# First mixer: row totals divided out on GpSimd ahead of the transposes, in a two-block transformer kernel

## The chip, the cores and the metric

One core of a Trainium2 chip runs the whole program. The metric is the device time of one execution in microseconds (us); the kernel before took 2069.79 us (median of 3 runs, 2069.43 to 2070.5).

## What is computed

The input is one sequence of 512 rows of width 1024. It goes through a first block of two layers and a second block of one layer. Every layer has a mixer (attention with 12 heads of 64 values, or a relative of it, and 4 heads of cross attention over 256 memory rows) and feed-forward parts. The change is in the mixer of the first layer, and there in the softmax of both kinds of head:

```python
def causal_block_attention(q, k, v, log_decay=None):
    ...
        logits = jnp.einsum('bhqd,bhkd->bhqk', qc, k).astype(jnp.float32)
        ...
        p = jax.nn.softmax(logits, axis=-1).astype(v.dtype)
        return jnp.einsum('bhqk,bhkd->bhqd', p, v)

def memory_cross(qm, k_mem, v_mem, q_gain, k_gain):
    ...
    p = jax.nn.softmax(logits, axis=-1).astype(v_mem.dtype)
    return jnp.einsum('bhsm,bmhd->bshd', p, v_mem).reshape(b, s, MEM_WIDTH)
```

## The kernel before

All matrix products with weights are done in three passes: each factor is split into a high part of the type fp32r and the remainder, and high by high, low by high and high by low are summed in PSUM. The weights come in units of four 128x128 tiles (RAW, by DMA), ACT makes the high part (WH, L2387) and DVE the remainder (WL, L2101). In the first mixer the projections from the normed input are steps called "wide" (L1944 to L1946, 256 columns a matmul) and the output projection `w_out` is a row of steps called "dense" (L1926 to L1928, 512 columns a matmul, three matmuls for one weight tile).

Attention is done in jobs of two heads (class `Pair`). The first mixer has eight jobs: two on the memory (two units each, of two 128-row query tiles by 256 keys) and six causal ones (three units each: query tiles 0 and 1 with 128 and 256 keys, tile 2 with 384, tile 3 with 512 keys). That is 22 units. A unit goes through these steps, for the heads x = 0 and 1:

- `pscore` (PE): scores into two PSUM banks (L2025 and L2032, the causal mask at L2015);
- `pmax` (DVE, L2211): the negated maximum of each row;
- `pexp` (ACT, L2457): the exponents into the buffer PP (four of them in turn) and, by the accumulator read that goes with each, the row totals into PSTAT;
- `pturn` (PE, L2044): transposes of 128x128 blocks of PP into the banks that held the scores. Head x waits for the exponents of head x;
- `pcopya` (DVE, L2233) and `pcopyb` (ACT, L2464): the transposed blocks into PT (two buffers);
- `pvals` (PE, L2058): values times PT, summed in PSUM bank 6, 64 array columns for each head.

Once the last unit of a job has its exponents, the division by the totals is made ready: `precip` (DVE, L2243) takes 8 reciprocals, `pwide` (GpSimd, L2622) spreads them over a 128x512 tile, `pbcast` (PE, L2068) transposes that tile in four blocks into a PSUM bank, `pspread` (ACT, L2480) copies it to TMP, `pmul` (DVE, L2248) multiplies bank 6 by it, ACT rounds the product into AOH (L2469) and `pmix` (DVE, L2251) leaves the remainder in AOL. AOH and AOL are the right-hand side of `w_out`. The other two mixers use the same classes.

The order of the program is made in two stages. `Pairs.run` is a generator: for each unit it gives out the scores of unit n+1, then the values of unit n-1, then the transposes of unit n, and `beat` interleaves this with the projection's steps at a set pace (0.65 beside the projections from the input, 1.5 beside `w_out`). Steps that follow are put off by `after`. Then the class `Arranged` goes through all steps with a cost for each (the class `Trial`) and rearranges PE, DVE and ACT: of the next 6 parts of PE (16 of DVE and ACT, 1 of GpSimd) it takes one that can begin, keeping steps of one kind in order. For PE it takes the earliest in the list that begins at most 0.15 us late by its costs. The result is a fixed order; on the chip every engine works through its own in order. The cost of a copy on GpSimd is 0.1 + n/650 us there, and a signal from GpSimd is counted as landing after 0.2 us.

Of the kernel before, what the change touches and what calls it, by code (L numbers as in the profile page):

```python
# [9 lines left out]
ALU = mybir.AluOpType  # L10
ACT = mybir.ActivationFunctionType
# [182 lines left out]
class Trial:  # L194
# [49 lines left out]
        return self.took(0.12 + size_of(out) / 960)  # L244

    def tensor_scalar(self, out, a, x, y, op0, op1=None):
        return self.took(0.12 + size_of(out) / 960)

    def tensor_reduce(self, out, a, axis, op, negate=False):
# [242 lines left out]
class Step:  # L492
# [37 lines left out]
    "pspread": ("pspread.act",),  # L530
    "pmul": ("pmix.mul", "pmix.act"),
    "pmix": ("pmix.dve",),
    "memload": (),
    "project": ("project.dve",),
    "conv": ("conv.act", "conv.dve"),
# [29 lines left out]
def program(nc, io):  # L565
    with ExitStack() as ctx:
# [471 lines left out]
        class Pairs:  # L1038


            def __init__(self, jobs, free):
                self.jobs, self.free, self.at = jobs, free, {}
                self.id = n_att[0]
                n_att[0] += 1

# [9 lines left out]
            def score(self, n, u):  # L1055
                job, key, jkey = self.jobs[n], (self.id, n, u), (self.id, n)
                if u == 0:
                    pstats.take(jkey, [("pwide.pool", jkey)])
                self.at[key] = t = Unit(job.units[u], pick_pair(att_ring), job.spare)
                held.update(t.banks)  # L1060
                for x, b in enumerate(t.banks):
                    psum.take(("pscore", key, x), [("pexp.act", key + (x,))], b)
                step("pscore", key, job=job, u=u, t=t)
                S, tokens = PSTAT[pstats.of[jkey]], pstats.before[jkey]

                def rest():
                    need(job.roots[1] if job.roots else [])
                    for xs in ((slice(0, 2),) if t.joint else (slice(0, 1), slice(1, 2))):
                        step("pmax", key + (xs.start,), job=job, t=t, xs=xs, S=S, tile=key, before=tokens)
                    if job.sealed(u) and job.sink is not None:  # L1070
                        step("psink", jkey, job=job, S=S, last=key + (0 if t.joint else 1,))
                    after(0.8 if job.spare else 0, exponents)

                def exponents():
                    free = []
                    for n_ in range(t.parts):
                        t.P.append(pp.take(("pp", key, n_), [("pturn.pe", key + (x,)) for x in range(2) if t.shared or x == n_]))
                        free += pp.before["pp", key, n_]
                    for x in range(2):
                        step("pexp", key + (x,), job=job, t=t, x=x, S=S, P=t.of(PP, t.P, x), before=tokens, src=PS[t.banks[x]],  # L1080
                             turned=free, top=("pmax.dve", key + (0 if t.joint else x,)))
                after(0.4, rest)
                return 0.4 + 1.4 * t.width / 512

            def turn(self, n, u):
                job, key = self.jobs[n], (self.id, n, u)
                need([("pexp.act", key + (1,))])
                t = self.at[key]
                t.copied = [("pcopy.act", key + (1,))] + ([] if t.shared else [("pcopy.dve", key + (0,))])
                for n_, b in enumerate(t.banks[0:t.parts]):  # L1090
                    psum.take(("pturn", key, n_), t.copied if t.shared else [x for x in t.copied if x[1][-1] == n_], b)
                for x in range(2):
                    step("pturn", key + (x,), t=t, P=t.of(PP, t.P, x), out=t.of(PS, t.banks, x),
                         before=psum.before["pturn", key, x] if x < t.parts else [])
                held.difference_update(t.banks)

                def copies():
                    if job.sealed(u):
                        self.recip(n)
                    free = []  # L1100
                    for n_ in range(t.parts):
                        t.PT.append(pt.take(("pt", key, n_), [("pvals.pe", key)]))
                        free += pt.before["pt", key, n_]
                    if t.shared:
                        both = lambda bufs, at: bufs[at[0]][:, :].rearrange("p (x k) -> p x k", x=2)[:, :, 0:t.width]
                        step("pcopyb", key + (1,), src=both(PS, t.banks), dst=both(PT, t.PT), free=free, turned=key + (1,))
                    else:
                        for x in range(2):
                            step(("pcopya", "pcopyb")[x], key + (x,), src=t.of(PS, t.banks, x), dst=t.of(PT, t.PT, x), free=free,
                                 turned=key + (x,))  # L1110
                after(0.5 if job.spare else 0.6, copies)
                return 0.25 * t.width / 128

            def values(self, n, u):
                job, key, jkey, ckey = self.jobs[n], (self.id, n, u), (self.id, n), (self.id, self.jobs[n].chunk)
                t = self.at[key]
                need(t.copied)
                if u == 0:
                    psum.take(("pvals", jkey), [("pmix.mul", ckey)], 6)
                step("pvals", key, job=job, u=u, jkey=jkey, t=t)  # L1120
                return 0.3 * t.width / 128

            def sums(self, n, i):
# [20 lines left out]
            def mix(self, n):  # L1144
# [4 lines left out]
                step("pmul", key, last=self.end(n), F=F, h=h, free=free)  # L1149
                after(1.2, lambda: step("pmix", key, F=F, h=h, l=l))  # L1150

            def older(self, scored, turned):

                ends = turned and self.jobs[turned[0]].sealed(turned[1])
                late = ends and self.jobs[turned[0]].spare
                cost = self.sums(*turned) if ends and not late else 0
                cost += self.values(*turned) if turned else 0
                cost += self.turn(*scored) if scored else 0
                return cost + (self.sums(*turned) if late else 0)
# [381 lines left out]
        for p in range(6):  # L1541
# [1 line left out]
            jobs.append(Pair([(qh[r, :], ql[r, :]) for r in (lo, hi)], [(kh[r, :], kl[r, :]) for r in (lo, hi)],  # L1543
                             VP[p // 2 % 2][:, :, 128 * (p % 2):128 * (p % 2) + 128], CAUSAL, p, pair_got[p],
                             cum=(2 * p, 2 * p + 1), wants=3))
        att = Pairs(jobs, fox_free)
        atts.append(att)
        side.append(att.run())
        pace[0], aux_ring[:] = 0.65, [2, 3, 4, 5, 7]
# [360 lines left out]
        def tensor(pe):  # L1910
            w = pe if trial(pe) else Once(pe)
            for s in turns(pe, "pe"):
# [125 lines left out]
                elif k == "pturn":  # L2038
                    for t in a["before"]:
                        w.wait_ge(*done(*t))  # L2040
                    w.wait_ge(*done("pexp.act", key))
                    for x in range(a["t"].width // 128):
                        c = slice(128 * x, 128 * x + 128)
                        p = pe.transpose(a["out"][:, c], a["P"][:, c], IDENT)  # L2044
# [40 lines left out]
        def vector(dve):  # L2085
# [6 lines left out]
            for s in turns(dve, "dve"):  # L2092
# [136 lines left out]
                elif k == "pcopya":  # L2229
                    for t in a["free"]:  # L2230
                        w.wait_ge(*done(*t))
                    w.wait_ge(*done("pturn.pe", a["turned"]))
                    dve.tensor_copy(a["dst"], a["src"]).then_inc(done.sem("pcopy.dve"), 1)  # L2233
                elif k == "precip":
                    St = a["S"]
                    for x in range(2):
# [138 lines left out]
        def scalar(act):  # L2375
# [3 lines left out]
            for s in turns(act, "act"):  # L2379
# [80 lines left out]
                elif k == "pcopyb":  # L2460
                    for t in a["free"]:
                        w.wait_ge(*done(*t))
                    w.wait_ge(*done("pturn.pe", a["turned"]))
                    act.activation(a["dst"], a["src"], ACT.Copy).then_inc(done.sem("pcopy.act"), 1)  # L2464
                elif k == "pmul":
                    for t in a["free"]:
                        w.wait_ge(*done(*t))
# [78 lines left out]
        def gpsimd(pool):  # L2546
# [31 lines left out]
            for s in turns(pool, "pool"):  # L2578
# [25 lines left out]
                elif k == "krope":  # L2604
                    w.wait_ge(*done("rtab.pool", 0))
                    w.wait_ge(*done(*a["got"]))
                    A, B = (x[:, :, :].rearrange("p (t h) f -> p t h f", t=4)[:, :, 0, :] for x in MLA_ROT)
                    M = [RS[x][:, 0:128].rearrange("p (t f) -> p t f", t=4) for x in range(2)]
                    turned(KRT[:, :, :], A, B, M, KRO[:, :, :]).then_inc(done.sem("krope.pool"), 1)
                    w.wait_ge(*done("krope.pool", 0))  # L2610
                elif k == "trope":
                    w.wait_ge(*done("rtab.pool", 0))
                    for t in a["got"]:
                        w.wait_ge(*done(*t))
                    w.wait_ge(g_in.sem, g_in.n)
                    turned(a["y"], a["A"], a["B"], a["M"], a["y"]).then_inc(done.sem("trope.pool"), 1)
                    w.wait_ge(*done("trope.pool", key))
                elif k == "pwide":
                    for t in a["before"]:
                        w.wait_ge(*done(*t))  # L2620
                    w.wait_ge(*done("precip.dve", key))
                    pool.tensor_copy(a["inv"][:, :].rearrange("p (i x d) -> p i x d", i=4, x=2),  # L2622
                                     a["S"][:, :, 3, :].rearrange("p x i -> p i x").unsqueeze(3).broadcast_to(
                                         [128, 4, 2, 64])).then_inc(done.sem("pwide.pool"), 1)
                elif k == "zero":
                    pool.memset(HX[key][:, 0:30], 0.0).then_inc(done.sem("zero.pool"), 1)

# [154 lines left out]
```

## Time and profile before

| What | Before |
|---|---|
| median of 3 runs | 2069.79 us |
| the profiled execution | 2069.65 us |
| its span, first to last instruction | 2067.9 us |
| PE busy | 2052.2 us |
| DVE busy | 1284.6 us |
| ACT busy | 966.0 us |
| GpSimd busy | 39.2 us |

The profiled execution took 0.14 us less than the median, and 1.75 us of its time lie outside its span. Matmuls are pipelined and their ends are modelled, so a matmul's row shows some 0.27 us where the next one starts 0.1 us later; the cost of a group of matmuls is read from start to start.

### The profile page before, as it was taken

Reading aid. Unit: us, or ns where it says so; the run is one execution under the profiler, and the core shown is the slowest. Engines: PE = TensorE matmul, PEld = TensorE weight load, DVE = VectorE, ACT = ScalarE, POOL = GpSimd, SP = SyncE. Lnnn points to the kernel's source line nnn. Section 1 sums busy time; section 2 is a strip of 40 time slices with the busy share of each in tenths; the row PEclk is TensorE's granted clock in tenths of the full one; section 3 lists DMA queues with packets and bytes.
Section 4 is the critical chain, followed back from the end, with each engine's and each line's share of the span. In section 5 each row is a group of like instructions: output and inputs, shape, how many; then the busy total and the mean of one; then the engine's idle time right before and its main releaser. Section 6 shows DMA issues by size and latency. Waiting matters only on the chain.

```text
span 2067.9 us, 29799 instructions
## 1 busy us (share of the span) xinstructions
PE 2052.2 (99%) x11018; PEld 1725.1 (83%) x11018; DVE 1284.6 (62%) x2111; ACT 966.0 (47%) x1883; POOL 39.2 (2%) x86
## 2 busy tenths in 40 slices
PE   8999999999999999999999999999999999999999
PEld 8998788888889788888888888888889878888887
DVE  7656688547756977774577555344548995544542
ACT  7655465334446865543344433223344764322331
POOL 0000001000000000000000000000001000000000
PEclk9999999999999999999999999999999999999999
DMA  6212233333323112333333333333332123333332
GB/s 220 68 47 62 62 97 97 97 97 97 97 90 98 45 36 63 92 99 97 96 97 98 97 96 97 97 97 97 97 94 75 37 82 95 97 98 96 98 101 87
DMA packets 101809, 185.51 MB, mean 90 GB/s; under 512 B 11552, under 2 KB 15008, under 8 KB 101408
## 3 DMA queue, kind: packets, MB, share of 16 engines
q1 hardware_dynamic: 101664, 183.61, 29.4%
q8 instruction: 87, 1.43, 0.3%
q14 instruction: 58, 0.48, 0.1%
HBM read 181.47 MB, written 2.10 MB: 89 GB/s over the span
## 4 chain that ended last, share of the span: by engine, by line
PE 97%; ACT 2%; DVE 1%; issue 0%; DMA 0%; POOLq 0%; DVEq 0%; ACTq 0%
PE PSA L1926 26%; PE PSA L1928 25%; PE PSA L1927 25%; PE PSA L1944 3%; PE PSA L1945 3%; PE PSA L1946 3%; PE PSA L2058 2%; PE PSA L2032 2%; PE PSA L2044 2%; PE PSA L1986 1%; ACT PP L2457 1%; PE PSA L2015 0%; PE PSA L2068 0%; PE PSA L2025 0%; PE PSA L1959 0%
## 5 line engine op out<-in xcount | busy, mean ns | idle before, releaser
L2387 ACT ACTIVATE WH<-RAW 128x512 fp32r<-128x512 f32 (+2 forms) x681 | 426.9, 628 | 810.6 <-PE PSA L1928 680.9
L2101 DVE TENSOR_TENSOR WL<-RAW,WH 128x512 fp32r<-128x512 f32 (+2 forms) x681 | 468.0, 688 | 390.9 <-ACT WH L2387 369.3
L1926 PE MATMUL PSA<-HNh,WH 128*128 128x512 f32 x1440 | 562.5, 391 | 0.0
L1928 PE MATMUL PSA<-HNh,WL 128*128 128x512 f32 x1440 | 560.3, 389 | 0.0
L1927 PE MATMUL PSA<-HNl,WH 128*128 128x512 f32 x1440 | 560.2, 389 | 0.0
L1927 PEld LDWEIGHTS PSA<-HNl,WH 128*128 128x128 f32 x1440 | 270.3, 188 | 57.0 <-issue 1.2
L1926 PEld LDWEIGHTS PSA<-HNh,WH 128*128 128x128 f32 x1440 | 270.3, 188 | 57.0 <-issue 1.2
L1928 PEld LDWEIGHTS PSA<-HNh,WL 128*128 128x128 f32 x1440 | 270.3, 188 | 56.4
L1926 PE MATMUL PSA<-Gh,WH 128*128 128x512 f32 x704 | 273.9, 389 | 0.0
L1927 PE MATMUL PSA<-Gl,WH 128*128 128x512 f32 x704 | 273.9, 389 | 0.0
L1928 PE MATMUL PSA<-Gh,WL 128*128 128x512 f32 x704 | 273.9, 389 | 0.0
L2124 DVE TENSOR_TENSOR PSA<-PSA,ACC 128x512 f32<-128x512 f32 x180 | 125.5, 699 | 166.6 <-PE PSA L1928 158.6
L1944 PE MATMUL PSA<-WH,HNh 128*128 128x256 f32 (+2 forms) x512 | 152.2, 297 | 6.1 <-DVE WL L2101 6.1
L1928 PEld LDWEIGHTS PSA<-Gh,WL 128*128 128x128 f32 x704 | 132.1, 188 | 27.5
L1927 PEld LDWEIGHTS PSA<-Gl,WH 128*128 128x128 f32 x704 | 132.1, 188 | 27.4
L1926 PEld LDWEIGHTS PSA<-Gh,WH 128*128 128x128 f32 x704 | 132.1, 188 | 27.4
L1945 PE MATMUL PSA<-WH,HNl 128*128 128x256 f32 (+2 forms) x512 | 148.1, 289 | 0.0
L1946 PE MATMUL PSA<-WL,HNh 128*128 128x256 f32 (+2 forms) x512 | 148.0, 289 | 0.0
L2089 DVE SCALAR_TENSOR_TENSOR CV<-PSA,PAR,CV 128x511 f32<-128x511 f32 (+1 forms) x176 | 131.9, 749 | 12.0 <-ACT CV L2486 3.4
L1944 PEld LDWEIGHTS PSA<-WH,HNh 128*128 128x128 f32 x512 | 99.0, 193 | 7.4 <-DVE HNl L2089 6.1
L1945 PEld LDWEIGHTS PSA<-WH,HNl 128*128 128x128 f32 x512 | 99.0, 193 | 0.2
L1946 PEld LDWEIGHTS PSA<-WL,HNh 128*128 128x128 f32 x512 | 98.8, 193 | 0.0
(267 smaller groups left out, 2206.5 us busy)
## 6 DMA issues: line engine op xcount, KB each, us to landing
RAW<-in_w SPq DMA_DIRECT2D x659, 256.0 KB, 2.6
XT<-in_x SPq DMA_DIRECT2D x8, 256.0 KB, 5.4
MT<-in_mem SPq DMA_DIRECT2D x2, 1024.0 KB, 5.3
out_x<-XT SPq DMA_DIRECT2D x8, 256.0 KB, 2.1
RAW<-in_w SPq DMA_DIRECT2D x8, 208.0 KB, 2.3
RAW<-in_w SPq DMA_DIRECT2D x6, 192.0 KB, 2.8
RAW<-in_w SPq DMA_DIRECT2D x8, 134.0 KB, 4.8
PAR<-in_par SPq DMA_DIRECT2D x1, 207.0 KB, 3.6
```

The lines of the kernel that those rows point to most:

```text
L1926: pe.matmul(out, wh, xh, start=(a["start"] and c == 0), stop=False)
L1927: pe.matmul(out, wh, xl, start=False, stop=False)
L1928: p = pe.matmul(out, wl, xh, start=False, stop=ends)
L1944: pe.matmul(out, h[:, c], wh, start=(a["start"] and t % a["share"] == 0), stop=False)
L1945: pe.matmul(out, l[:, c], wh, start=False, stop=False)
L1946: p = pe.matmul(out, h[:, c], wl, start=False, stop=(a["stop"] and t % a["share"] == a["share"] - 1))
L2032: p = pe.matmul(PS[tile.banks[x]][:, col:col + nk], job.q[x][qx][:, qs], job.k[x][kx][:, ks], start=(opens and n == 0 and m == 0), stop=(( ...
L2044: p = pe.transpose(a["out"][:, c], a["P"][:, c], IDENT)
L2089: ins = dve.scalar_tensor_tensor(*x)
L2101: dve.tensor_tensor(l, r, h, ALU.subtract).then_inc(done.sem("split.dve"), 1)
L2124: dve.tensor_tensor(ps, ps, nm.acc, ALU.mult).then_inc(done.sem("scale.dve"), 1)
L2387: act.activation(h, r, ACT.Copy).then_inc(done.sem("split.act"), 1)
```

## The change

In the first mixer (`Pairs(jobs, fox_free, True)`) each unit's exponents are multiplied by the reciprocals of their rows' totals in place. After both heads' exponents DVE takes the reciprocals of this unit's rows (`pshare`), then GpSimd multiplies PP by them (`pnorm`, one `tensor_scalar` for each query tile and head), and the transposes wait for `pnorm` instead of `pexp`. `precip`, `pwide`, `pbcast`, `pspread` and `pmul` are not given out there. ACT rounds bank 6 itself into AOH (`pout`) and `pmix` takes the remainder from bank 6, which is free again after `pmix` (before: after `pmul`). The two other mixers keep the steps of before. `Trial` gets a cost for `tensor_scalar` on GpSimd.

```diff
     def tensor_scalar(self, out, a, x, y, op0, op1=None):
+        if self.name == "pool":
+            return self.took(0.1 + size_of(out) / 650)
         return self.took(0.12 + size_of(out) / 960)
...
             def score(self, n, u):
...
-                    pstats.take(jkey, [("pwide.pool", jkey)])
+                    pstats.take(jkey, [("pnorm.pool", self.end(n) + (1,)) if self.early else ("pwide.pool", jkey)])
...
+                    if self.early:
+                        after(0.8, shares)
+
+                def shares():
+                    step("pshare", key, S=S, rows=t.rows)
+                    for x in range(2):
+                        step("pnorm", key + (x,), t=t, x=x, S=S, P=t.of(PP, t.P, x))
...
             def turn(self, n, u):
-                need([("pexp.act", key + (1,))])
+                need([("pnorm.pool" if self.early else "pexp.act", key + (1,))])
...
-                         before=psum.before["pturn", key, x] if x < t.parts else [])
+                         before=psum.before["pturn", key, x] if x < t.parts else [],
+                         got="pnorm.pool" if self.early else "pexp.act")
...
-                    if job.sealed(u):
+                    if job.sealed(u) and not self.early:
                         self.recip(n)
...
-                    psum.take(("pvals", jkey), [("pmix.mul", ckey)], 6)
+                    psum.take(("pvals", jkey), [("pmix.dve" if self.early else "pmix.mul", ckey)], 6)
                 step("pvals", key, job=job, u=u, jkey=jkey, t=t)
+                if self.early and job.sealed(u):
+                    after(0.2, lambda: self.out_of(n))
...
+            def out_of(self, n):
+                job, key = self.jobs[n], (self.id, self.jobs[n].chunk)
+                free = self.free(job.chunk)
+                need(free)
+                F, h, l = PSA[:, 6, :], AOH[:, job.chunk, :], AOL[:, job.chunk, :]
+                step("pout", key, last=self.end(n), F=F, h=h, free=free)
+                after(0.8, lambda: step("pmix", key, F=F, h=h, l=l))
...
-                ends = turned and self.jobs[turned[0]].sealed(turned[1])
+                ends = turned and self.jobs[turned[0]].sealed(turned[1]) and not self.early
...
-        att = Pairs(jobs, fox_free)
+        att = Pairs(jobs, fox_free, True)
...
+                elif k == "pshare":
+                    St, rows = a["S"], a["rows"]
+                    for x in range(2):
+                        w.wait_ge(*done("pexp.act", key + (x,)))
+                    dve.reciprocal(St[:, :, 3, rows], St[:, :, 1, rows]).then_inc(done.sem("pshare.dve"), 1)
...
+                elif k == "pout":
+                    for t in a["free"]:
+                        w.wait_ge(*done(*t))
+                    w.wait_ge(*done("pvals.pe", a["last"]))
+                    act.activation(a["h"], a["F"][:, :], ACT.Copy).then_inc(done.sem("pmix.act"), 1)
...
+                elif k == "pnorm":
+                    w.wait_ge(*done("pshare.dve", key[:-1]))
+                    for i, col, k0, nk, masks in a["t"].subs:
+                        z = pool.tensor_scalar(a["P"][:, col:col + nk], a["P"][:, col:col + nk],
+                                               a["S"][:, a["x"], 3, i:i + 1], None, ALU.mult)
+                    z.then_inc(done.sem("pnorm.pool"), 1)
```

## Rows read from the trace of the kernel before

**Rows 1.** The page: busy time by engine, and the chain that ended last.

```profile
PE 2052.2 (99%) x11018; PEld 1725.1 (83%) x11018; DVE 1284.6 (62%) x2111; ACT 966.0 (47%) x1883; POOL 39.2 (2%) x86
...
PE 97%; ACT 2%; DVE 1%; issue 0%; DMA 0%; POOLq 0%; DVEq 0%; ACTq 0%
```

**Rows 2.** Busy time by stretch: start:end, length, PE, PEld, DVE, ACT, POOL, PEclk, DMA, GB/s.

```profile
60.00:240.00 180.00, 180.00 (x1597) 159.30 (x1596) 108.88 (x205) 105.40 (x279) 4.91 (x8) 1.00 0.19 55
```

**Rows 3.** What PE waited for in the whole span: us, times, longest us.

```profile
PE PSA L1944 <- DVE WL L2101: 6.1, 1, 6.1
PE PSA L2044 <- ACT PP L2457: 4.4, 6, 1.9
```

**Rows 4.** Timeline of PE (start us, us, operation, count): L2068, and the values behind.

```profile
82.55 0.66 PE L2068 MATMUL PSA<-CONST,TMP 128*128 128x128 f32 x4
83.14 1.09 PE L2058 MATMUL PSA<-PT,VMEM 128*64 128x128 f32 x16
...
121.91 0.61 PE L2068 MATMUL PSA<-CONST,TMP 128*128 128x128 f32 x4
122.45 1.09 PE L2058 MATMUL PSA<-PT,VP 128*64 128x128 f32 x16
```

**Rows 5.** PE's groups of instructions from 60 to 240 us, by shape: L2068.

```profile
L2068 PE MATMUL PSA<-CONST,TMP 128*128 128x128 f32 x32 | 4.9, 275 | 0.0
```

**Rows 6.** Timeline of PE: the first wide matmul behind values, and the next two.

```profile
143.57 0.38 PE L1944 MATMUL PSA<-WH,HNh 128*128 128x256 f32 x1
...
144.03 0.28 PE L1944 MATMUL PSA<-WH,HNh 128*128 128x256 f32 x1
144.38 0.28 PE L1944 MATMUL PSA<-WH,HNh 128*128 128x256 f32 x1
```

**Rows 7.** GpSimd's groups by shape: operation, shapes, count, busy us, mean ns, idle before.

```profile
L2573 POOL TENSOR_TENSOR RT<-YC,Q_ROT 128x128 f32<-128x128 f32 x8 | 4.5, 584 | 24.2 <-ACT SQ L2429 24.2
L2598 POOL TENSOR_TENSOR Q_ROT<-TMP,PAR 128x32 f32<-128x32 f32 x16 | 4.4, 304 | 0.0
...
L2587 POOL TENSOR_SCALAR TMP<-TMP 128x96 f32<-128x96 f32 x1 | 0.5, 467 | 97.0 <-ACT TMP L2508 97.0
L2566 POOL CAST CONST<-PT 128x140 fp32r<-128x140 f32 x1 | 0.3, 303 | 0.0
```

**Rows 8.** Timelines of GpSimd and DVE: one spread copy with a subtraction beside it.

```profile
88.02 0.61 POOL L2622 COPY TMP<-PSTAT 128x512 f32<-128x512 f32 x1 [12.22 <-DVE PSTAT L2243]
88.20 0.97 DVE L2251 TENSOR_TENSOR AOL<-TMP,AOH 128x512 fp32r<-128x512 f32 x1 [0.25 <-ACT AOH L2469]
...
103.18 0.69 DVE L2251 TENSOR_TENSOR AOL<-TMP,AOH 128x512 fp32r<-128x512 f32 x1 [0.23 <-ACT AOH L2469]
```

**Rows 9.** Timeline of ACT: the last exponents of two units.

```profile
102.34 0.19 ACT L2457 ACTIVATION_READ_ACCUMULATOR PP<-PSA,PSTAT 128x1 f32 x1
...
210.50 0.20 ACT L2457 ACTIVATION_READ_ACCUMULATOR PP<-PSA,PSTAT 128x1 f32 x1
```

**Rows 10.** Timeline of PE: the transposes of these units; then the last values.

```profile
108.91 0.88 PE L2044 MATMUL PSA<-CONST,PP 128*128 128x128 f32 x6
...
210.83 1.09 PE L2044 MATMUL PSA<-CONST,PP 128*128 128x128 f32 x8
...
231.48 1.09 PE L2058 MATMUL PSA<-PT,VP 128*64 128x128 f32 x16
```

**Rows 11.** DVE's groups from 60 to 240 us: the product with the spread totals, the reciprocals.

```profile
L2248 DVE TENSOR_TENSOR TMP<-PSA,TMP 128x512 f32<-128x512 f32 x8 | 5.5, 691 | 5.0 <-PE PSA L2058 5.0
L2243 DVE RECIPROCAL PSTAT<-PSTAT 128x8 f32<-128x8 f32 x8 | 1.6, 203 | 6.7 <-ACT PP L2457 6.7
```

**Rows 12.** Timeline of DVE at the mixer's end: last remainder, two additions of projection sums.

```profile
234.11 0.68 DVE L2251 TENSOR_TENSOR AOL<-TMP,AOH 128x512 fp32r<-128x512 f32 x1
...
238.96 0.69 DVE L2257 TENSOR_TENSOR XT<-PSA,XT 128x512 f32<-128x512 f32 x1 [1.25 <-PE PSA L1928]
247.87 0.69 DVE L2257 TENSOR_TENSOR XT<-PSA,XT 128x512 f32<-128x512 f32 x1 [2.01 <-PE PSA L1928]
```

More of the change, by code:

```diff
@@ L532 @@
     "pmix": ("pmix.dve",),
+    "pshare": ("pshare.dve",),
+    "pnorm": ("pnorm.pool",),
+    "pout": ("pmix.act",),
     "memload": (),
@@ L1038, in program, with __init__ @@
         class Pairs:
-            def __init__(self, jobs, free):
-                self.jobs, self.free, self.at = jobs, free, {}
+            def __init__(self, jobs, free, early=False):
+                self.jobs, self.free, self.at, self.early = jobs, free, {}, early
                 self.id = n_att[0]
@@ L2040, in tensor @@
                         w.wait_ge(*done(*t))
-                    w.wait_ge(*done("pexp.act", key))
+                    w.wait_ge(*done(a["got"], key))
                     for x in range(a["t"].width // 128):
```

## The prediction

> **What bounds the kernel.** The page comes first: PE is busy for 99% of the span and carries 97% of the chain that ended last; DVE and ACT have a third to a half of the time free and GpSimd nearly all [rows 1]. So only what PE does, or waits for, can change the time. The second view is the table of busy time by stretch. The first mixer's attention lies between 60 and 240 us; there PE shows 180.00 of 180 us busy at full clock, DVE 108.88, ACT 105.40, GpSimd 4.91 [rows 2]. The third is the list of what PE waited for. It holds six waits of transposes for exponents, 4.4 us together, and one wait for weights of 6.1 us at the start [rows 3]. Since the second view shows no idle PE from 60 to 240 us, none of these to speak of is in the stretch that is changed. Modelled ends could cover short stalls there, so I also followed the starts on PE's timeline: between 60 and 256 us each group starts when the group before has had its usual time, and what is over are switches between full and half array (some 0.1 us each, below). PE is saturated there: work taken off it is a gain of its own size, delay elsewhere costs nothing as long as PE finds other work.
>
> **What is removed from PE.** Each of the eight jobs loses its four transposes of spread reciprocals, 32 in all [rows 5]. The cost is read from start to start: 83.14 - 82.55 = 0.59 us at one place, 122.45 - 121.91 = 0.54 us at another [rows 4]. The eight places read 0.59, 0.54, 0.54, 0.53, 0.54, 0.52, 0.53 and 0.53 us, 4.3 us together. They stand mostly between a unit's scores and an older unit's values, both of which use half the array, so the switch goes with them. **Term 1: -4.3 us.** No other step of PE is added or dropped; transposes of exponents, scores and values keep their number.
>
> **What is removed and added elsewhere.** DVE loses eight products of 0.691 us and eight reciprocals of 0.203 us, 7.1 us [rows 11]; it gets 22 reciprocals of two or four columns, at most 0.203 us each, 4.5 us. ACT loses eight copies of the spread tile. Rounding and remainder stay, with PSUM as source. All this is beside PE and costs nothing; the cover is PE's own work. GpSimd loses eight spread copies and gets 80 multiplications: for a causal job two each of 128, 256, 384 and 512 columns, for a memory job eight of 256. No DMA is moved, and none waits on these steps.
>
> **The price of one multiplication.** The trace has no such instruction of this width. From below: the spread copy of 512 columns takes 0.61 us [rows 8] and the cast of 140 takes 0.303 [rows 7], a slope of 0.31/372 = 0.83 ns a column. From above: products of two tensors take 0.304 us for 32 columns and 0.584 for 128 [rows 7], 2.9 ns a column, 1.70 us for 512. The nearest row by kind is the one multiplication by a scalar, 96 columns in 0.467 us [rows 7]; with the copies' slope that gives 0.49, 0.60, 0.71 and 0.81 us for 128, 256, 384 and 512 columns. I take these, since there is one tensor input as in a copy. A unit then costs GpSimd 2.2, 1.4 and 1.6 us (causal, in order) or 2.4 us (memory), 41 us in all over 180: it does not become the bound.
>
> The Trainium skill bears on this choice. Its page "GPSIMD Engine Reference" (Elementwise — side-by-side cycle accounting) puts ordinary elementwise work at about 2.6 cycles an element on GpSimd, a floor that it gives for two inputs, and the best loops at 1.8, with 512 elements in 769 ns. By the first figure, at the 1.2 GHz of that page, a 512-column multiplication would be an estimated 1.1 us and more, by the second close to what I took. The spread copy here, at 0.61 us for 512 columns, is quicker than both.
>
> **The new wait and who is behind it.** The transposes now wait for reciprocals and two multiplications. After the last exponents come some 0.3 us for the reciprocal with its signals and 1.4 to 2.4 us of GpSimd: about 2.4 us later than before for head 1, and more for head 0, which used to go ahead of head 1's exponents. How long did transposes lie ready? A unit in the middle has its last exponents at 102.34 + 0.19 and is turned at 108.91, 6.4 us later; one of the fifth causal job has 210.70 and 210.83, hardly anything [rows 9, 10]. Over the 22 units I count 12 with under 3 us (three of the four memory units, three of the third and fourth causal jobs, all six of the last two). There a static order as before would stall PE by about 2 us each. But the order is made anew by `Arranged`, which leaves a late transpose at the head of its six parts and takes wide or dense tiles past it. There is enough to take: the last values start at 231.48 [rows 10] and their remainder is done at 234.79, yet the first sum that needs them is added at 247.87, with twelve tiles between it and the addition at 238.96 [rows 12]. So the tail has over 10 us of cover. The stall that remains is what the planner misjudges. It counts 0.1 + n/650 us: 1.58, 1.38, 1.78 and 1.98 us a unit against my 2.2, 1.4, 1.6 and 2.4. The excess, 0.6 us for two tight first units and 0.4 for three memory units, is 2.4 us, and a late transpose falls on average into the middle of a tile, which hides most of it. **Term 2: +0.7 us** (bounds 0 and the second rival's 13).
>
> **Array switches.** Values that come ready later may no longer stand directly behind scores. Leaving a values group costs the next wide step 0.46 us (143.57 to 144.03) in place of 0.35 (144.03 to 144.38) [rows 6], and entering about the same, so a separated group costs 0.2 us. Two or three such, **term 3: +0.5 us** (bounds -0.5, if the new order joins groups, and +2, ten groups).
>
> **Other things held longer.** Bank 6 is freed by `pmix`, so after a rounding and a subtraction instead of one product: about 1.5 us later. Next values come 5 us and more after, no price. PP and score banks are kept 2.4 us longer; four PP buffers are two units, and scores of unit n+2 come after the transposes of unit n anyway. GpSimd and DVE get in each other's way: the subtraction that ran beside a spread copy took 0.97 us, not 0.69, 0.28 more for 0.43 us of overlap, and the copy kept its 0.61 [rows 8]. With 41 us of GpSimd and about a fifth of DVE's time in such two-input instructions, DVE pays some 6 us of its 71 free ones. No price, as PE's weights are split well ahead.
>
> **Sum:** -4.3 + 0.7 + 0.5 = -3.1 us. The profiled execution would go from 2069.65 to 2066.6; it stands 0.14 us under the median, so the forecast for the median is 2069.79 - 3.1 = 2066.7 us. A measurement of this kernel tells about 0.2% (4.1 us) from no change, so this counts as the same.
>
> **Rivals.**
> - *All of it is kept*: the planner's price of GpSimd is at or above the true one, no stall, no lost switch. For it: the copy is quicker than the planner counts (0.61 against 0.89). Against it: the small instructions look dearer. 2069.8 - 4.3 = 2065.5 us, just past the 0.2% line; with joined groups 2065.0. Chance 0.25.
> - *GpSimd is slow* (slower than before): a multiplication costs what a product of two tensors does. A unit is then 3.1, 2.7, 3.4 or 3.8 us, 1.3 to 1.9 us over plan, and PE, in order, waits at each of the 12 tight places: 18.6 us, less some 6 hidden in tiles, so about +13 - 4.3 = 2078 us. It decides from about 0.7 us of stall at each of 12 places, which is 1.2 to 1.3 us for 512 columns. For it: the two-tensor rows. Against it: one tensor input only. Chance 0.10.
> - *The delay eats the gain*: reciprocals stand behind other work on DVE and are slowed by GpSimd, score banks are held and PE finds the next step of its kind blocked. Half the places cost 0.7 us: +4, 2069.7 us, between 2068 and 2072. For it: the last two jobs have no slack and tight spacing. Against it: the cover counted above. Chance 0.15.
> - *The forecast*, 2065.9 to 2068: chance 0.50.
>
> That the change is without effect on PE is excluded: the 32 transposes go.
>
> **Chances and range.** Faster by over 0.2% is most of the first rival and an edge of the forecast: 0.25. Slower by over 0.2% is the second and a little of the third: 0.12. The rest, 0.63, is within. The range leaves out the second rival and a margin below the first: 2065.0 to 2072.0 us.
>
> **What would show it.** Right: L2068 has 32 matmuls less, none from 60 to 240 us; GpSimd gains about 36 us; multiplications of 512 columns take near 0.8 us; PE from 60 to 240 us has waits of under 1.5 us for GpSimd; the stretch up to the first feed-forward part ends 3 us earlier and all behind it is unchanged. Wrong: waits of transposes on GpSimd of several us, 512 columns at 1.2 us or more, or time that moves in stages after the first mixer.

## The result, and the profile after

| Kernel | Median | Ratio to before, 95% interval |
|---|---|---|
| before | 2069.79 us (5 runs, 2069.33 to 2070.50) | |
| changed | 2088.22 us (5 runs, 2086.36 to 2090.42) | 1.0085 [1.0075, 1.0096] |

The change made the kernel 18.4 us slower by the medians. The forecast was 2066.7 us, range 2065.0 to 2072.0, and slower had a chance of 0.12. The profiled execution took 2086.36 us with a span of 2084.6 us, 16.7 more than before; it was the fastest of the five, so the account below explains 16.7 us, and the other 1.7 us of the median have no trace.

The page first: busy time by engine of the changed kernel. It answers to [rows 1].

```profile
PE 2053.8 (99%) x10986; PEld 1722.1 (83%) x10986; DVE 1283.3 (62%) x2118; ACT 962.0 (46%) x1875; POOL 102.8 (5%) x142
```

PE has 32 matmuls less, as forecast. GpSimd gained 64 us where I had priced some 36. Next the table of busy time by stretch of the changed kernel (start:end, length, then PE, PEld, DVE, ACT, POOL, granted clock, DMA share, GB/s); it answers to [rows 2].

```profile
60.00:90.00 30.00, 27.70 (x260) 25.66 (x258) 20.10 (x45) 20.39 (x61) 12.93 (x13) 1.00 0.17 54
90.00:140.00 50.00, 50.00 (x482) 45.31 (x481) 28.33 (x55) 28.02 (x75) 20.71 (x20) 1.00 0.18 53
140.00:190.00 50.00, 45.84 (x421) 40.41 (x421) 24.75 (x47) 26.03 (x70) 17.46 (x16) 1.00 0.16 50
190.00:240.00 50.00, 43.94 (x311) 34.73 (x312) 26.35 (x54) 22.00 (x59) 14.14 (x14) 0.93 0.16 48
```

PE was never idle from 60 to 240 us before. Now it is idle for 2.3 us beside the memory jobs, for 4.2 beside the third and fourth causal jobs and for 6.1 beside the last two, where the granted clock is 0.93 too. From 90 to 140 us, where exponents used to lie ready for five us and more, nothing is lost. The list of what PE waited for in the changed kernel names the cause; it answers to [rows 3].

```profile
PE PSA L2067 <- POOL PP L2661: 13.3, 16, 2.2
PE PSA L1967 <- DVE WL L2124: 6.8, 2, 6.1
PE PSA L2067 <- ACT PP L2485: 4.4, 6, 1.9
PE PSA L2055 <- ACT PT L2492: 1.4, 2, 0.7
PE PSA L1967 <- DVE XT L2112: 0.8, 1, 0.8
```

L2067 are the transposes, L2661 the multiplications: 16 waits, 13.3 us. Their durations, from GpSimd's groups by shape, stand beside [rows 7].

```profile
L2661 POOL TENSOR_SCALAR PP<-PP,PSTAT 128x256 f32<-128x256 f32 x28 | 27.5, 991 | 59.7 <-DVE PSTAT L2261 59.7
L2661 POOL TENSOR_SCALAR PP<-PP,PSTAT 128x512 f32<-128x512 f32 x12 | 19.0, 1598 | 28.4 <-DVE PSTAT L2261 28.4
L2661 POOL TENSOR_SCALAR PP<-PP,PSTAT 128x384 f32<-128x384 f32 x12 | 14.8, 1242 | 7.1 <-DVE PSTAT L2261 7.1
...
L2661 POOL TENSOR_SCALAR PP<-PP,PSTAT 128x128 f32<-128x128 f32 x12 | 7.5, 628 | 66.1 <-DVE PSTAT L2261 66.1
```

512 columns take 1.60 us, not the 0.81 that I took; the slope is (1598 - 628)/384 = 2.5 ns a column. GpSimd's rows are rough, but the timeline of GpSimd, where neighbours are merged into one row from the first start to the last end, gives nearly the same: two of 512 columns in 3.10 us, four of 256 in 3.64 us, two each of 128 and 256 in 2.98 us.

```profile
83.00 3.64 POOL L2661 TENSOR_SCALAR PP<-PP,PSTAT 128x256 f32<-128x256 f32 x4 [3.25 <-DVE PSTAT L2261]
...
96.47 2.98 POOL L2661 TENSOR_SCALAR PP<-PP,PSTAT 128x128 f32<-128x128 f32 x4 [3.19 <-DVE PSTAT L2261]
...
111.72 3.10 POOL L2661 TENSOR_SCALAR PP<-PP,PSTAT 128x512 f32<-128x512 f32 x2 [4.61 <-DVE PSTAT L2261]
```

(The row at 96.47 merges both widths under the first.) Where did the time go, in place? The sum of squares for the feed-forward part stands right behind the changed stretch, and the start of its first matmuls is a mark that can be read in every kernel. PE's timeline before, then changed:

```profile
271.40 1.02 PE L1969 MATMUL PSA<-ACC,ONE 128*128 128x512 f32 x2
...
286.91 1.02 PE L1992 MATMUL PSA<-ACC,ONE 128*128 128x512 f32 x2
```

That is +15.5 us. The first matmul of the second memory projection starts at 639.8 and 656.5, +16.7; the end of the span is +16.7. So 15.5 us are lost in the changed stretch, 1.2 between the two marks, near the second mixer, and nothing later.

### The profile page after: what moved, and what is told of

It reads as the page before. It is cut to its first block, busy times and chain, and to the rows that moved or that the text cites. A ratio compares the mean times of both kernels' runs of the same rounds, so it can differ in the third digit from the quotient of the medians.

```text
span 2084.6 us, 29827 instructions
## 1 busy us (share of the span) xinstructions
PE 2053.8 (99%) x10986; PEld 1722.1 (83%) x10986; DVE 1283.3 (62%) x2118; ACT 962.0 (46%) x1875; POOL 102.8 (5%) x142
## 4 chain that ended last, share of the span: by engine, by line
PE 94%; ACT 2%; POOL 1%; DVE 1%; DMA 1%; issue 1%; SPq 0%; POOLq 0%; DVEq 0%; ACTq 0%
PE PSA L1949 25%; PE PSA L1951 25%; PE PSA L1950 25%; PE PSA L1967 3%; PE PSA L1968 3%; PE PSA L1969 3%; PE PSA L2055 2%; PE PSA L2081 2%; PE PSA L2067 2%; POOL PP L2661 1%; PE PSA L2009 1%; ACT PP L2485 1%; PE PSA L2038 0%; DVE PSTAT L2234 0%; DMA MT<-in_mem 0%
## 5 line engine op out<-in xcount | busy, mean ns | idle before, releaser
L1949 PE MATMUL PSA<-HNh,WH 128*128 128x512 f32 x1440 | 562.5, 391 | 0.0
L1949 PEld LDWEIGHTS PSA<-HNh,WH 128*128 128x128 f32 x1440 | 270.3, 188 | 57.0 <-issue 1.2
L1949 PE MATMUL PSA<-Gh,WH 128*128 128x512 f32 x704 | 273.9, 389 | 0.0
L1949 PEld LDWEIGHTS PSA<-Gh,WH 128*128 128x128 f32 x704 | 132.1, 188 | 27.4
```

The lines of the kernel that those rows point to most:

```text
L1949: pe.matmul(out, wh, xh, start=(a["start"] and c == 0), stop=False)
```

## Experiments

Each ran on the same chip as its own runs of the kernel before; ratios are given with their 95% intervals. The median of before was 2070.28 us beside one_block, short_mults, planned_true and mults_on_dve, 2070.18 beside true_reach16, dve_by_head, gpsimd_middle_jobs and dve_first_six, and 2070.14 beside changed_reach16, dve_reach16 and dve_six_reach16. Two theories stood at first: (1) GpSimd's multiplications are longer than planned for, and PE stands in its fixed order; (2) some other part of the change costs, whatever GpSimd takes.

### One block: what the removed work is worth

```diff
                 elif k == "pbcast":
...
-                    for i in range(4):
+                    for i in range(4 if trial(pe) or key[0] else 1):
```

> The kernel before in its own order, but in the first mixer only one of the four blocks of spread reciprocals is transposed (three quarters of the multiplier tile are then old PSUM contents). It prices the work taken off PE: 24 transposes of 0.107 us are 2.6 us. Theory (PE saturated, work removed is gained at its own size): 2067.2 us, ratio 0.9988. Rival (PE's pace is set by something else there): no change, 2069.8 us.

2067.69 us, ratio 0.9987 [0.9978, 0.9996]: 2.6 us less than before, by 24 transposes of 0.108 us. The mark behind the stretch agrees:

```profile
268.60 1.02 PE L1969 MATMUL PSA<-ACC,ONE 128*128 128x512 f32 x2
```

It stands 2.8 us earlier than before, so the rival (no change) is out: PE is saturated there, and work that is taken off it is gained at its own size. By 0.108 us each, 32 are worth 3.45 us. That the switch of each of the eight groups makes up the rest of the 4.3 is not shown by this run, which keeps one transpose in each group; dve_reach16, below, bears on it.

### Short multiplications in the same order

```diff
-                        z = pool.tensor_scalar(a["P"][:, col:col + nk], a["P"][:, col:col + nk],
+                        n = nk if trial(pool) else 16
+                        z = pool.tensor_scalar(a["P"][:, col:col + n], a["P"][:, col:col + n],
                                                a["S"][:, a["x"], 3, i:i + 1], None, ALU.mult)
```

> The changed kernel with the same planned order on every engine, but each GpSimd multiplication does only the first 16 columns of its query tile (the rest of the exponents stays undivided, so this leaves out most of the division). Theory 1 (GpSimd's real multiplications, 0.63 to 1.60 us, are longer than the planner's price, and PE stands still in its fixed order): each falls to 0.3 to 0.5 us, PE's waits for GpSimd fall from 13.3 us to under 1 us and the time to 2065 to 2067 us, 3 to 5 us below the kernel before. Theory 2 (another part of the change costs, whatever GpSimd takes: bank 6 held until the remainder, transposes of head 0 waiting for head 1, DVE's reciprocals): the time stays above 2078 us.

2070.72 us, ratio 1.0001 [0.9992, 1.0011]. The order of every engine is that of the changed kernel, so the length of the multiplications alone is worth 2088.2 - 2070.7 = 17.5 us: theory 1. Theory 2 wanted over 2078 us and is out. But 2065 to 2067 was missed too, since not all of the rest comes back. The lists of waits and of GpSimd's groups of this kernel:

```profile
PE PSA L1967 <- DVE WL L2124: 6.6, 2, 6.2
PE PSA L2067 <- ACT PP L2485: 4.5, 6, 1.9
PE PSA L2067 <- POOL PP L2662: 2.0, 2, 1.1
PE PSA L2055 <- ACT PT L2492: 1.4, 2, 0.7
PE PSA L1967 <- DVE XT L2112: 0.8, 1, 0.8
...
L2662 POOL TENSOR_SCALAR PP<-PP,PSTAT 128x16 f32<-128x16 f32 x64 | 23.0, 380 | 188.3 <-DVE PSTAT L2261 188.2
```

Even at 0.38 us each, the first transposes of the last two jobs wait 1.0 us each for multiplications: these begin only when both heads have their exponents, and the order put nothing in between. The mark behind the stretch in this kernel:

```profile
270.30 1.02 PE L1992 MATMUL PSA<-ACC,ONE 128*128 128x512 f32 x2
```

It is 1.1 us earlier than before. Of that, -4.3 were forecast for the removed work, +2.0 are these waits and +0.2 one for DVE at 74.7 us; by difference some +1.0 is left for array switches and waits too short to show. The 1.2 us near the second mixer come on top, and the span ends 0.1 us under that of before.

### The planner told the truth

```diff
         if self.name == "pool":
-            return self.took(0.1 + size_of(out) / 650)
+            return self.took(0.33 + size_of(out) / 410)
```

> The changed kernel with only the planner's price of a GpSimd multiplication set to what the trace shows, 0.33 + n/410 us in place of 0.1 + n/650; the instructions are the same, PE, DVE and ACT get another order. Theory 1a (the misjudged price alone cost the time; there is other work to put in): PE's waits for GpSimd under 2 us, time 2065 to 2068 us. Theory 1b (the chain through GpSimd is too long for the last two jobs; no order fills it, since projection tiles and scores stand in line behind buffers and banks that the late transposes hold): still 2073 us or more, with PE idle in the last two jobs, from about 205 to 250 us.

2081.15 us, ratio 1.0051 [1.0036, 1.0066]. Theory 1a falls: the true price takes back only 7 of the 18 us. Theory 1b fits so far. PE's timeline of this kernel ahead of the last causal job's first transposes:

```profile
226.33 0.34 PE L2055 MATMUL PSA<-FKH,FQL 64*128 64x384 f32 x2
226.60 0.28 PE L2038 MATMUL PSA<-CB 128*128 128x128 bf16 x2
230.72 0.87 PE L2067 MATMUL PSA<-CONST,PP 128*128 128x128 f32 x3 [3.84 <-POOL PP L2661]
231.24 0.77 PE L1949 MATMUL PSA<-AOH,WH 128*128 128x512 f32 x1
```

PE stands for 3.84 us before a transpose, and directly behind that transpose comes a tile of the output projection (L1949), which multiplies the outputs of older jobs. Why was it not taken first? That gave a third theory (1c): the planner's list of six parts was full of attention steps that all waited on the same chain. A list of 16 in the kernel before gives the identical program, so the length of the list by itself costs or gains nothing there.

### A longer list

```diff
-        arranged.append(Arranged(trials, ("dve", "act", "pe"), {"pe": 6, "dve": 16, "act": 16, "pool": 1}, chains))
+        arranged.append(Arranged(trials, ("dve", "act", "pe"), {"pe": 16, "dve": 16, "act": 16, "pool": 1}, chains))
```

> As planned_true (true price of the multiplications), and the planner may look 16 parts ahead on PE instead of 6. The same change of 6 to 16 in the kernel before gives that kernel's own order on every engine again, so the reach by itself changes nothing there. Theory 1c (the six parts were full of attention steps that waited, with projection tiles ready behind them): PE keeps working through the last two jobs, waits for GpSimd under 2 us, 2067 to 2072 us. Rival (the tiles behind are themselves blocked by banks, weights or the emission order): as planned_true, 2079 to 2083 us.

2069.41 us, ratio 0.9997 [0.9987, 1.0006]. What PE waited for in this kernel:

```profile
PE PSA L1967 <- DVE WL L2124: 6.1, 1, 6.1
PE PSA L2067 <- ACT PP L2485: 4.4, 6, 1.9
PE PSA L2055 <- ACT PT L2492: 1.4, 2, 0.7
PE PSA L1967 <- DVE XT L2112: 0.8, 1, 0.8
PE PSA L2067 <- POOL PP L2661: 0.8, 2, 0.5
```

Waits for GpSimd fell from 7.6 us (in planned_true) to 0.8, with multiplications as long as ever. So the longer chain can be covered, and theory 1b falls too; it was the short list that hid the cover. What stood in the six parts at each wait is not shown. The fourth combination is the low price with the long list:

> The changed kernel with only the planner's reach on PE raised from 6 to 16 parts; the price stays too low (0.1 + n/650). It completes the table of price and reach. Theory (both faults count, and reach is the larger: it let the blocked steps fill the list; the low price leaves waits of about 1 us where a transpose is placed as early as it was thought ready): between true_reach16 and the changed kernel, 2073 to 2078 us, PE's waits for GpSimd 4 to 10 us. Rival A (reach alone explains it): 2069 to 2071 us. Rival B (the low price alone decides): 2084 us or more.

2082.39 us, ratio 1.0056 [1.0042, 1.0070]; I had expected 2073 to 2078. Its waits for GpSimd are 10.9 us, in 14 places:

```profile
PE PSA L2067 <- POOL PP L2661: 10.9, 14, 2.2
```

| | list of 6 | list of 16 |
|---|---|---|
| price 0.1 + n/650 | 2088.2 | 2082.4 |
| price 0.33 + n/410 | 2081.2 | 2069.4 |

Either mend alone brings 6 to 7 us, both together 19. The reading that fits: with the low price a transpose is put in too early, however long the list; with the short list a rightly priced transpose still finds no tile to be put behind. The expectation that the reach was the larger fault was wrong: the two are of a size, and each hides the other.

### The same multiplications on DVE

```diff
-    "pnorm": ("pnorm.pool",),
+    "pnorm": ("pnorm.dve",),
...
+                        z = dve.tensor_scalar(a["P"][:, col:col + nk], a["P"][:, col:col + nk],
+                                               a["S"][:, a["x"], 3, i:i + 1], None, ALU.mult)
```

> The changed kernel with the multiplications on DVE in place of GpSimd (same steps, DVE priced at 0.12 + n/960 us by the planner). Theory 1 (the length of GpSimd's multiplications): DVE does 512 columns in 0.4 to 0.7 us, a unit costs under 1.4 us, PE waits little, 2065 to 2068 us. Theory 2 (other parts of the change): above 2075 us. If DVE gets too full, waits for WL or for maxima appear and the time lies between, 2068 to 2074 us.

2069.26 us, ratio 0.9995 [0.9986, 1.0005]. DVE's groups from 60 to 262 us of this kernel:

```profile
L2265 DVE TENSOR_SCALAR PP<-PP,PSTAT 128x256 f32<-128x256 f32 x28 | 8.8, 348 | 0.0
...
L2265 DVE TENSOR_SCALAR PP<-PP,PSTAT 128x512 f32<-128x512 f32 x12 | 5.5, 483 | 0.2
```

DVE does 512 columns in 0.48 us where GpSimd takes 1.60. With the short list and the changed kernel's steps, 19 us are back, though the 2065 to 2068 us expected were missed; 1.7 us of waits in the last two jobs remain (two, 1.0 at most), like those of the short multiplications. I tried to remove them by giving each head its own reciprocals:

> As mults_on_dve, and each head has its own reciprocal, so that head 0 is multiplied and transposed without waiting for head 1's exponents. Theory (of what is left in mults_on_dve above the sum of removed work, 1.7 us is two waits of first transposes in the last two jobs for multiplications that wait for both heads): those waits go, 2067.5 to 2068.5 us. Rival (22 more small DVE instructions take back what it gives): 2069 to 2070.5 us.

2069.07 us, ratio 0.9995 [0.9986, 1.0005], no difference that can be told: the wait before the last job's first transposes went from 0.78 us to 0.82, and that of the job before is now 0.95 us for the exponents themselves. So waiting for both heads was not what cost the time. The next kernel is mults_on_dve with the long list:

> As mults_on_dve with a reach of 16 parts. Theory (its two waits of 1.7 us before the first transposes of the last two jobs have the same cause, a full list): they go, 2067 to 2068.5 us. Rival (they come from DVE being later than planned): 2069 to 2070 us.

2068.10 us, ratio 0.9988 [0.9979, 0.9998]. By the medians alone this can't be told from mults_on_dve, but the two waits are gone, as the list of this kernel shows (DVE's multiplications are not in it):

```profile
PE PSA L1967 <- DVE WL L2124: 6.2, 1, 6.2
PE PSA L2067 <- ACT PP L2491: 4.5, 6, 1.9
PE PSA L2055 <- ACT PT L2498: 1.4, 2, 0.7
PE PSA L1967 <- DVE XT L2112: 0.8, 1, 0.8
PE PSA L2055 <- DVE PT L2256: 0.2, 1, 0.2
PE PSA L2091 <- POOL TMP L2661: 0.2, 1, 0.2
```

and the mark behind the stretch is at 267.57 us, where mults_on_dve has 269.93:

```profile
267.57 1.02 PE L1992 MATMUL PSA<-ACC,ONE 128*128 128x512 f32 x2
```

It is 3.8 us earlier than before. So the removed work is worth nearly the 4.3 us that were forecast once nothing waits, with 0.5 us left for switches; 1.2 us go again near the second mixer.

### Only some of the jobs

The flag `early` became a tuple of job numbers (0 and 1 are the memory jobs, 2 to 7 the causal ones), and `self.early` the test `n in self.early`. This kernel also has the right price, so it is compared with planned_true:

```diff
-            return self.took(0.1 + size_of(out) / 650)
+            return self.took(0.33 + size_of(out) / 410)
...
-        att = Pairs(jobs, fox_free, True)
+        att = Pairs(jobs, fox_free, (2, 3, 4, 5))
```

> GpSimd multiplications only in the first four causal jobs, with the true price in the planner; the two memory jobs and the last two causal jobs divide as before. Theory (the loss sits in the memory jobs and the last two causal jobs, which have no slack between exponents and transposes): four of the eight gains of 0.54 us are kept, less 1.2 us lost in another order near the second mixer and some 1 us of waits in the third and fourth causal job: 2069 to 2071 us. Rival (every job loses): 2075 us or more.

2070.42 us, ratio 1.0003 [0.9994, 1.0013], with 0.3 us of waits for GpSimd. With the other four jobs dividing as before, the loss of planned_true (2081.2 us) is gone: with the right price and the short list it sits in the memory jobs and the last two causal ones. With the low price the third and fourth causal jobs lose too, 4.2 us of idle PE in the changed kernel; that split was not run. The next kernel has the multiplications of jobs 0 to 5 on DVE, with the short list:

> As mults_on_dve for the first six jobs; the last two causal jobs divide as before. Six of eight gains of 0.54 us, 3.2 us, without the two waits of 1.7 us together, less up to 1.2 us near the second mixer: 2067 to 2068.5 us. Rival (the gain is lost in array switches and order all the same): 2069.5 us or more.

2067.81 us, ratio 0.9988 [0.9979, 0.9997]: six of the eight groups of transposes are gone, without the waits. With the long list as well:

> As dve_first_six with a reach of 16 parts; the version that should be best. dve_first_six shows no waits that the kernel before has not, but for 0.8 us near the second mixer, so there is little for the reach to give: 2067 to 2068.3 us, ratio 0.9985 to 0.999. Rival: the memory jobs gain too, 2066.5 us.

2067.88 us, ratio 0.9991 [0.9982, 1.0000]. The three best versions (dve_reach16, dve_first_six and this one) lie 2.0 to 2.4 us below the kernel before by their medians, two of them clear of 1 by their intervals, and can't be told from each other. The gain over the kernel before is small, 0.1%.

## Why the prediction was wrong, point by point

- **PE bounds, and removed work is gained at its own size: right.** one_block shows it for 24 of the 32 transposes. The mark of dve_reach16, 3.8 us earlier than before, bears -4.3 us out to within the 0.5 us of term 3.
- **The price of one multiplication: wrong, and the first step that failed.** I put 512 columns between 0.61 and 1.70 us and took 0.81, by the rule that one tensor input makes it like a copy. It measured 1.60, with the slope of 2.5 ns that products of two tensors suggested (2.9) and not the copy's 0.83. (The text counts 80 multiplications; its own list gives 64, and 64 ran. Its 41 us go by the 64.) The row that I trusted, 96 columns in 0.467 us, was near the truth (the new slope gives 0.55 for 96) but could not give a slope. A unit cost 3.0, 2.5, 3.1 or 3.6 us where the second rival had said 3.1, 2.7, 3.4 and 3.8; and 1.60 is past the 1.2 to 1.3 from which I had said it decides. The page "GPSIMD Engine Reference" of the Trainium skill (Elementwise — side-by-side cycle accounting) gives about 2.6 cycles an element, for two inputs, and I set that figure aside because the copy was quicker. The multiplication, with one tensor input, took slightly more than that: 2.5 ns are 3.0 cycles at that page's 1.2 GHz. The 1.60 us for 512 columns lie above both the 1.1 us that I estimated from that figure and the 769 ns of the page's best loop.
- **"There is enough to take": wrong, the second step.** Cover there was, as true_reach16 shows. But I said that the planner leaves a late transpose at the head of six parts and takes tiles past it, and did not count what else stands in the six. Both heads' transposes, scores, values and the turning of queries for later jobs share the list, and a list whose six parts all wait takes no tile. That it was full of these is inferred; what is shown is that lengthening it leaves the kernel before as it is and takes 12 us off the changed kernel with the right price. This is the part of the loss that a right price leaves, 2081.2 against 2069.4.
- **Term 2, +0.7 us with 13 as the upper bound:** the waits for GpSimd alone are 13.3 us in 16 places (I had counted 12 tight ones), and they do not end it. After a wait of 1.98 us at 210.5 us and one of 0.46 at 213.7 the granted clock fell, though a wait of 2.18 us at 73.7 had left it at 1.00; the stretch from 210 to 220 us of the changed kernel reads:

```profile
210.00:220.00 10.00, 7.22 (x35) 4.64 (x35) 3.44 (x8) 3.06 (x9) 5.62 (x6) 0.70 0.10 28
```

  0.70 in the mean is 6 of 10 us at the lower level, 1.2 in place of 2.4 GHz. By the starts on PE's timeline, the matmuls that ran there at the lower level cost an estimated 2.6 us more than at the higher. So the 15.5 us of the stretch are -4.3, +13.3 of waits, about +2.6 of clock, and, by difference, some 4 of array switches and waits too short to be listed. That remainder is not located. The second rival had the mechanism, nearly the units' times and, with 18.6 less 6, even the sum of the waits: 13 us. Its 2078 us was 10 short of the median by what it did not count: the clock, the remainder of some 4 us, the 1.2 us near the second mixer and the 1.7 us by which the median lies further up than the trace.
- **Term 3, +0.5 us:** by difference some 1.0 us in the order of short_mults and 0.5 in that of dve_reach16, within the bounds given. In the changed kernel it can't be told from short waits; the two together are some 4 us, past the upper bound of 2.
- **"All behind it is unchanged": wrong by 1.2 us.** Every version of the change waits 0.8 us for DVE before the first tile of the second mixer's projection, where the kernel before does not wait. I left open why the order differs there; the steps are the same, and the cause is not shown.
- **No price for bank 6, for buffers, for DVE: right.** With the long list and DVE doing all multiplications, nothing of these shows among the waits of the first mixer.
- **The chances.** Slower had 0.12 because I gave the multiplication's price a value by analogy and only 0.10 to its other end. The duration of the multiplications decided whether the time fell into the range (with 16 columns each, in the very same order, it was 2070.7 us), both ends were in the trace, and no row was of its kind and width: the two ends deserved near equal chances.

## What to carry to other kernels

In a kernel whose bound engine is full and runs a fixed order, a longer chain beside it is free only if the order knows its length and can see past it; test both at once, since here each mend alone brought a third of what both brought together. Of work that is moved to another engine, the first thing to find is the duration of that very instruction at that width; here a copy on GpSimd, at 0.83 ns a column, said little of a multiplication on GpSimd, at 2.5. Taking 32 short transposes off the full engine was worth 3.8 us at best; the waits of the longer chain were 0.8 us in the mean, and one in each of the eight jobs would already be more.

## What was not expected of the hardware

A GpSimd multiplication by a per-row scalar took 0.63, 0.99, 1.24 and 1.60 us for 128, 256, 384 and 512 columns of fp32, with one tensor input, where its spread copy takes 0.61 us for 512 in this mixer [rows 8] and 0.78 in the other two (14 copies of the changed kernel); DVE did the same multiplication of 512 columns in 0.48 us, 3.3 times quicker. And at 16 columns GpSimd still took 0.38 us.
